# A mixture-of-experts block on one core: the down weights move from SyncE's DMA ring to ScalarE's

## The reference

```python
def moe(h, ...):                       # t: 512 tokens x 1024
    scores = sigmoid(t @ w_router)     # 64 experts; 8 chosen per token, in 4 of 8 groups
    combine = ...                      # weight of each chosen expert, 0 elsewhere
    y = (silu(t @ w_sh_gate) * (t @ w_sh_up)) @ w_sh_down        # shared expert
    for g in range(N_GROUPS):          # w_gate, w_up: 1024 x 256; w_down: 256 x 1024, for each expert
        a = silu(t @ w_gate[sl]) * (t @ w_up[sl])
        y = y + (a * combine[:, sl]) @ w_down[sl]
    return y
x = x + moe(rms_norm(x))
x = x + sigmoid(rms_norm(x) @ w_ple_gate) * rms_norm(p @ w_ple_proj)
```

## Time and profile before

| | |
|---|---|
| Runs of the kernel before | 1147.06, 1151.31, 1151.76 us; median 1151.31 us |
| The profiled execution's own time | 1148.81 us |
| Its span, first to last instruction | 1147.1 us |
| Busy share of the span | TensorE 97%, weight load 80%, VectorE 74%, ScalarE 68%, GpSimd 36% |
| Granted TensorE clock | 0.999 |
| Bytes moved by DMA | 291.61 MB, of them 254.13 MB by q1 |
| Largest entry of the chain that ended last, after TensorE | DMA `arena<-in_w_exp_up`, 16% |

### The profile page before, as it was taken

The page is one execution under the profiler, slowest core; times in us unless marked ns, Lnnn a source line. Parts: engine busy times, 40 slices in busy tenths (PEclk is TensorE's granted clock), DMA queues, the critical chain, the costliest instruction groups (busy, mean ns, idle before and its releaser), DMA issues.

```text
span 1147.1 us, 17728 instructions
## 1 busy us (share of the span) xinstructions
PE 1108.6 (97%) x5459; PEld 913.1 (80%) x5459; DVE 853.9 (74%) x1211; ACT 784.2 (68%) x1266; POOL 414.0 (36%) x477
## 2 busy tenths in 40 slices
PE   7999999999899999999999999999999999999898
PEld 7888888788678886878888888878878888777577
DVE  3535533277764577999999999898889998899665
ACT  5734424367553334888899888788888888888662
POOL 1220000034374001455555554555545555544320
PEclk9999999999999999999999999999999999999999
DMA  6422422112303089999999999999999999999631
GB/s 242 148 74 73 146 73 73 41 49 70 144 2 129 19 329 362 382 318 370 391 384 387 384 390 390 371 363 378 381 365 375 372 378 372 364 375 326 183 121 74
DMA packets 71955, 291.61 MB, mean 254 GB/s; under 512 B 15139, under 2 KB 20550, under 8 KB 46950
## 3 DMA queue, kind: packets, MB, share of 16 engines
q1 hardware_dynamic: 52496, 254.13, 56.5%
q0 software_dynamic: 18768, 34.79, 12.2%
q10 hardware_dynamic: 646, 2.12, 0.5%
HBM read 284.61 MB, written 42.07 MB: 285 GB/s over the span
## 4 chain that ended last, share of the span: by engine, by line
PE 67%; DMA 17%; DVE 7%; ACT 4%; issue 4%; POOL 1%; SPq 0%; DVEq 0%; ACTq 0%; POOLq 0%
DMA arena<-in_w_exp_up 16%; PE bank L1940 7%; PE bank L1638 7%; PE bank L1942 6%; PE bank L1941 6%; PE bank L1674 6%; PE bank L1678 6%; PE bank L1675 6%; PE bank L1963 3%; PE bank L1961 3%; PE bank L1962 3%; PE bank L1906 3%; DVE arena_r L1529 2%; PE bank L1630 2%; PE bank L2031 1%
## 5 line engine op out<-in xcount | busy, mean ns | idle before, releaser
L1529 DVE TENSOR_TENSOR arena_r<-arena,win_r 128x1024 fp32r<-128x1024 f32 x252 | 291.9, 1219 | 44.6 <-ACT win_r L997 44.5
L997 ACT ACTIVATE win_r<-arena 128x1024 fp32r<-128x1024 f32 x252 | 246.2, 1058 | 46.9 <-DMA arena<-in_w_exp_up 46.8
L1940 PE MATMUL bank<-win_r,work_r 128*128 128x512 f32 x512 | 206.4, 403 | 14.9 <-DVE x_low_r L1488 13.9
L1941 PE MATMUL bank<-win_r,x_low_r 128*128 128x512 f32 x512 | 200.2, 391 | 0.0
L1942 PE MATMUL bank<-arena_r,work_r 128*128 128x512 f32 x504 | 197.7, 392 | 0.0
L680 POOL DMA_INDIRECT moe_sum<-ya,sidx x64 | 115.5, 1804 | 115.1 <-ACT ya L1030 100.4
L1503 DVE TENSOR_TENSOR arena_r<-arena,hT_r 128x1024 fp32r<-128x1024 f32 x128 | 150.3, 1214 | 0.0
L1940 PEld LDWEIGHTS bank<-win_r,work_r 128*128 128x128 f32 x512 | 96.6, 189 | 38.8 <-issue 20.5
L1674 PE MATMUL bank<-arena_r,hT_r 128*128 128x512 f32 (+2 forms) x320 | 122.2, 382 | 1.2 <-DVE win_r L1140 1.2
L1675 PE MATMUL bank<-arena_r 128*128 128x512 f32 (+2 forms) x320 | 120.9, 378 | 0.0
L1678 PE MATMUL bank<-win_r,hT_r 128*128 128x512 f32 (+2 forms) x320 | 120.8, 377 | 0.0
(11 more groups left out here) (290 smaller groups left out, 2222.5 us busy)
## 6 DMA issues: line engine op xcount, KB each, us to landing
arena<-in_w_exp_down SPq DMA_DIRECT2D x64, 1024.0 KB, 24.7
arena<-in_w_exp_gate SPq DMA_DIRECT2D x63, 1024.0 KB, 8.4
arena<-in_w_exp_up SPq DMA_DIRECT2D x63, 1024.0 KB, 24.7
win<-in_w_in SPq DMA_DIRECT2D x8, 2048.0 KB, 7.8
win<-in_w_o SPq DMA_DIRECT2D x2, 2048.0 KB, 7.8
arena<-in_w_ple_gate SPq DMA_DIRECT2D x2, 2048.0 KB, 28.1
arena<-moe_sum SPq DMA_DIRECT2D x8, 512.0 KB, 7.4
win<-in_mla_w_qb SPq DMA_DIRECT2D x4, 576.0 KB, 4.0
```

The source lines that it names most:

```text
L997: act.activation(gu_hi[n % 2][:, :, cols], raw[:, :, cols], ACT.Copy).then_inc(gu_hi_r, 1)
L1529: dve.tensor_tensor(low_[:, :, cols], raw[:, :, cols], gu_hi[n % 2][:, :, cols].bitcast(F32), ALU.subtract).then_inc(gu_lo_r, 1)
L1940: pe.matmul(b_, x_hi[:, k, :], w_hi, start=(k == 0), stop=False)
L1941: pe.matmul(b_, x_lo[:, k, :], w_hi, start=False, stop=False)
```

## The change

SyncE keeps the gate-up loads and loses the down loads from expert 4 on, with the waits for `dn_done` that stood before them. ScalarE gets them: in step j, after the four casts of gate-up of expert j+1, and after its waits for `w_dn` of expert j and for the down matmuls of expert j-2, it issues the down load of expert j+2, and goes on with the cast of down of expert j. The buffer is the one that expert j-2 has left. In further passes (not executed here) SyncE loads down of experts 0 to 3.

```diff
-            def expert_dn(e, r, one=True):
-                src = a["w_exp_down"][0][e] if one else a["w_exp_down"][0][bass.ds(e, 1)].rearrange("o d f -> (o d) f")
+            def expert_dn(e, r):
+                src = a["w_exp_down"][0][e]
                 sp.dma_start(arena[:, RB[r] + WGU:RB[r] + WEXP],
                              src.rearrange("(p k) f -> p (k f)", p=P)).then_inc(w_dn[r], 16)
...
                 if e != 2 * RING:
                     sp.wait_ge(gu_done, e - RING + 1)
                     expert_gu(e, e % RING)
-                sp.wait_ge(dn_done, e - RING)
-                expert_dn(e - 1, (e - 1) % RING)
             with sp.Fori(3, E // RING) as q:
                 for r in range(RING):
                     sp.wait_ge(gu_done, q * RING + (r - RING + 1))
                     expert_gu(q * RING + r, r, one=False)
-                    sp.wait_ge(dn_done, q * RING + (r - RING))
-                    expert_dn(q * RING + (r - 1), (r - 1) % RING, one=False)
-            sp.wait_ge(dn_done, E - RING)
-            expert_dn(E - 1, RING - 1)
...
             n_pass = act.value_load(nb_i, min_val=1, max_val=NPASS_MAX)
+            def expert_dn(q, j):
+                src = (a["w_exp_down"][0][j] if q is None else
+                       a["w_exp_down"][0][bass.ds(q * RING + j, 1)].rearrange("o d f -> (o d) f"))
+                act.dma_start(wdn[j % RING].rearrange("p k d -> p (k d)"),
+                              src.rearrange("(p k) f -> p (k f)", p=P)).then_inc(w_dn[j % RING], 16)
...
                     act.wait_ge(w_dn[j % RING], at(b, q, 4, 16 * (j // RING + 1)))
                     if not free or j >= 2:
                         act.wait_ge(dn_done, at(b, q, 1, j - 1))
+                    if not free or 2 <= j < E - 2:
+                        expert_dn(q, j + 2)
```

More of the change, by code:

```diff
@@ L495, in _ @@
                         expert_gu(e, e % RING)
-                        if e >= 1:
-                            sp.wait_ge(dn_done, b * E + (e - RING))
-                            expert_dn(e - 1, (e - 1) % RING)
+                        if e < RING:
+                            sp.wait_ge(dn_done, b * E + (e - RING + 1))
+                            expert_dn(e, e)
                     with sp.Fori(2, E // RING) as q:
@@ L502, in _ @@
                             expert_gu(q * RING + r, r, one=False)
[L503 to L506, removed]
             sp.dma_start(pbuf, a["p"][0, 0].rearrange("(t q) n -> q t n", q=P)).then_inc(ld_p, 16)
```

## The result

After the change the kernel takes 1151.84 us (median of 20 runs, 1148.74 to 1156.22); before, timed on the same chip, 1148.68 us (20 runs, one of which, at 1380.13 us, the ratio leaves out). The ratio is 1.0032 (95% interval 1.002 to 1.0044): 3.7 us slower, 2.3 to 5.1. By the bound of 0.5% that is the same, though the interval lies clear of no change. The profiled executions show the same difference, with spans of 1150.8 and 1147.1 us.

What follows compares the result with a forecast made beforehand. TensorE paced the early experts, the slowest DMA engines the later ones. (1.9 + 0.7) down loads x 2.6 us = 6.8 us, other terms 0, on 1148.81 gave 1155.6, put at 1157 us; range 1149 to 1166.

Steps and rivals of the forecast that it cites:

- the second case of rival C: Row scatters in q0: late because rows get a third of an engine's turns; slack some 16 us; no own price.
- rival C: Expert steps: slower by a wait, from colliding issuers (15 us beside the shift, 1173 us) or late scatters; chance 0.10.
- SyncE's waits, 0: SyncE's loads: dropping the dn_done waits gains 0, since gate-up loads still wait for gu_done.
- ScalarE's issue, 0: ScalarE's 60 down issues: hidden behind the fourth gate-up cast, price 0, at most 0.45 us a step.
- the hole: Start of q1, 489.9 to 506.6 us: down of expert 7, issued later, takes gate-up's time; 0.7 of a down load.
- The bound and both paces: Experts: TensorE paces 9.36 us, then slowest DMA engines about 9.95 us an expert; both paces stay unchanged.
- rival B: Slow DMA engines speed up if a single queue was the limit: 1128 us, or 1138 for half; chance 0.12.
- Down is served ahead: Down's own queue: down mostly served before gate-up, shifting the queue once by 1.9 down loads of 2.6 us.
- The forecast's other signs: Gate-up casts: DMA waits begin some experts earlier, total 5 to 8 us more; last in_w_exp_up lands near 1064 us.
- the forecast's shift: Gate-up's queue on the slowest engines: delayed once, not each step, by down loads served ahead; 6.8 us with the start's part.

Runs made afterwards that it cites:

- the pad pair: Kernels before and after, both without rows of tokens 256 to 511 but with a 0.5 MB copy for each expert (12 to 63): 1182.69 and 1182.60 us.
- a late issue: Changed kernel with ScalarE issuing the down load of expert j+2 behind silu of expert j: 1155.51 us, 1.0064 of the kernel before.

## Why the prediction was wrong in its wait and its size

The forecast was 1157 us, with 6.8 us for the change. Measured are 1151.84 us and 3.7 us. The time lies in the range and slower was held likelier than faster, but the sum had the wrong wait in it. What came was the second case of rival C, the late scatter, which had no price of its own; all of C had a chance of 0.10. That the time lies so near is in part luck.

**SyncE's waits, 0; ScalarE's issue, 0.** Right: the first stretch runs at 9.37 us an expert, with no idle "issue" ahead of L1003, and the pair with half of the rows agrees to the noise. The place was wrong. I put the issue behind the fourth cast of gate-up; in after it stands at 873.68 us, inside L1028 and ahead of L980 and the four casts, 3.4 us earlier than 2.9 us into the casts. At the start it is 501.67 us (ahead of casts that begin at 501.95) and not the 505.0 that the hole was worked out with, 0.8 us behind SyncE's old 500.89, and it landed in 5.2 us, at 506.9, about when the next gate-up was issued (506.43). So the 0.7 of a load for the hole has no support.

**The bound and both paces.** Right as to the paces: 9.37 us and then 9.94 an expert, before 9.37 and 9.92. DMA bounds both kernels, and not by the total of its bytes (rows laid differently: -1.5% with the same bytes); that it is by the slowest engines fits and is not seen directly. Nothing of rival B is seen.

**Down is served ahead.** Right as to down: it lands after 10.0 us, not 24.7. That gate-up is served later for it is shown nowhere: in the kernels as they are its landings at equal progress did not move, and the times of the pad pair are equal.

**The step that failed** is "where down is served": "1.9 down loads more before it than in the old order", all of them at the expense of gate-up, with q0 keeping its 8.3 and 9.4 us. Up to ScalarE's first wait gate-up lost nothing (largest landing 17.1 us, before 17.2), over the run the up weights landed sooner, after 18.9 us, and the rows paid: +7.3 us for gathers, +7.8 for scatters. I had weighed that under C as "a scatter that is late because rows get a third of an engine's turns", and set it aside with its 16 us of slack against 10.7, the greatest landing of before: a figure of the queue in the old arrangement, taken for the new one. It reached 17.2 at the median and 19.1 at most. The forecast's other signs fail with it: no wait of L993 where 5 to 8 us more were expected, and the last gate-up cast at 1059.43 us, not near 1064.

**The size.** The sum put 6.8 us ahead of the last landing and 0 behind it. The 0 was right: the chain has no DMA behind the experts. Of the 6.8 us, 3.4 are measured where TensorE starts the last gate-up, 3.7 at the end. The term of 0.7 of a load, 1.8 us, has no support. The term of 1.9 loads, 4.9 us, is near the 4.5 us of the expert before the last, but by coincidence: these are no loads ahead of gate-up, but five steps of 10.4 us instead of 9.6 when the scatters' slack had run out. From 4.5 us at the casts to 3.4 at TensorE it falls in the last step, where before waits 2.15 us for its last up load and after waits for nothing.

The Trainium skill (DMA: Bandwidth & Descriptors, section "Issuing engines are not separate DMA queues") has issue time as the only thing that several issuing engines save. For the pair with half of the rows that agrees with the times, 1128.96 and 1130.65 us. In the kernels as they are, the landings of three queues moved by 5.8 to 14.7 us, and the measurement decides: the issuing engine also chooses a queue, and here that decided who is late. That each engine takes turns packet by packet (same page, "Queues, rings and completion order") would give such an exchange; it is argued, not shown, since the one run that changed the size of the packets moved the first wait by one expert and the time by nothing.

**Open:** how the DMA engines divide their time between the three queues; why the five steps at the end of the slack cost more each than those behind them; why a late issue costs 3.7 us more; and whether the forecast's shift exists where weights are what is late.

## What to carry to other kernels

When DMA is the bound, as here, don't expect a stream to gain by a queue of its own: its own loads landed sooner, and the lateness came out in another queue. Ask of each queue how late its transfers may be before someone waits, and let it grow in the one with the most slack. Here that is the weights' ring, with 27 us, and not the rows, with 16. And don't judge a queue's slack by the landings of the old arrangement; price it at what the others could leave it. Where the rows of an indirect DMA lie was worth more than either arrangement of the weights: 17 us.

## What the runs showed of the hardware that was not expected

- ScalarE's instruction stream ran well ahead of its engine: the issue at 873.68 us stands in the program behind L980 and four casts that ended at 878.1 us.
- A third busy queue nearly doubled the landing of indirect DMAs at a DMA share of 1.01 to 1.02 (gather 8.3 to 15.6, scatter 9.4 to 17.2 us), and added 1.3 to 2.0 us at one of 0.96 to 0.99.
- Which of the 128 slots an expert's rows lie in, with the same bytes, was worth 1.5% (1131.68 us). That this is a matter of which DMA engine serves which slot is the reading of it; no view here shows a single engine's load.
